# A Hyena spectrum stage on one core: each PSUM evacuation and product over two or four neighbouring banks in one instruction

## The reference, cut to what matters

```python
def long_conv(u, hf, bias):
    seqlen = u.shape[1]
    uf = jnp.fft.rfft(u, n=2 * seqlen, axis=1)
    y = jnp.fft.irfft(uf * hf[None], n=2 * seqlen, axis=1)[:, :seqlen]
    return y + u * bias

def hyena(p, lp, rows, row_len):
    ...
    hf = hyena_filters(seqlen, lp)
    z = x1 * long_conv(v, hf[:, 0], bias[0])
    z = x2 * long_conv(z, hf[:, 1], bias[1])
    return z * jax.nn.silu(p['z_b'].astype(f32))
```

## Time and profile before

| what | value |
|---|---|
| median of 3 runs | 5350.56 us (5349.45 to 5352.09) |
| the profiled execution's own time | 5330.26 us |
| its span | 5328.6 us |
| mean granted TensorE clock | 0.962 of full speed |
| busy share of the span: PE, DVE, ACT, POOL | 89%, 36%, 24%, 21% |
| matmuls | 27121 |

### The profile page before, as it was taken

One profiled execution on the slowest core, in us unless ns is written; L12 is line 12 of the kernel. 1 busy time (PEld: TensorE's weight loads), 2 busy tenths in 40 slices (PEclk: granted clock), 3 DMA queues, 4 the chain that ended last, 5 costly groups with the idle time before them and its releaser, 6 DMA issues. The chain is left out here.

```text
span 5328.6 us, 66000 instructions
## 1 busy us (share of the span) xinstructions
PE 4738.9 (89%) x27121; PEld 2951.7 (55%) x27121; DVE 1942.2 (36%) x2790; ACT 1264.8 (24%) x2707; POOL 1109.5 (21%) x1071
## 2 busy tenths in 40 slices
PE   6237999999999999999999799988888888499998
PEld 6113555555444444444444688876665555377676
DVE  0462333344862122100200466655555555212121
ACT  0101122211101111100110355545455454000000
POOL 0000000000000000000000899954333533011111
PEclk9968999999999999999999899999999999699999
DMA  2603113321341111122111777755454544713130
GB/s 105 206 0 127 43 48 88 81 62 52 105 114 56 52 55 59 48 101 79 60 47 55 220 210 210 207 161 195 152 196 160 185 172 152 261 64 126 63 126 24
DMA packets 440191, 602.92 MB, mean 113 GB/s; under 512 B 123536, under 2 KB 355400, under 8 KB 416968
## 3 DMA queue, kind: packets, MB, share of 16 engines
q1 hardware_dynamic: 407368, 530.79, 30.5%
q0 software_dynamic: 14112, 51.39, 3.5%
q10 hardware_dynamic: 18432, 16.79, 0.9%
HBM read 377.17 MB, written 221.70 MB: 112 GB/s over the span
## 5 line engine op out<-in xcount | busy, mean ns | idle before, releaser
L1002 PE MATMUL proj_b<-proj_hT,proj_wt 128*128 128x512 f32 (+1 forms) x5504 | 2312.5, 581 | 1.0 <-issue 0.7
L1002 PEld LDWEIGHTS proj_b<-proj_hT,proj_wt 128*128 128x128 f32 x5504 | 1047.5, 191 | 1213.2 <-issue 1201.9
L615 POOL DMA_DIRECT2D proj_wt<-in_w_in_dram x80 | 71.3, 892 | 2588.7 <-PE proj_b L1002 2401.5
L747 ACT ACTIVATE proj_rawx<-proj_b 128x512 f32<-128x512 f32 x192 | 114.8, 600 | 949.5 <-PE proj_b L1002 908.8
L749 ACT ACTIVATE proj_res<-proj_b 128x512 f32<-128x512 f32 x128 | 76.5, 597 | 788.0 <-PE proj_b L1002 788.0
L2241 PE MATMUL mrg_b<-mrg_za,mrg_w_a 128*128 128x256 f32 x1024 | 233.6, 381 | 27.4 <-DMA mrg_w_o<-in_w_out_dram 27.4
L860 DVE TENSOR_SCALAR proj_arena<-proj_rawx,proj_cw_hy 128x2048 f32<-128x2048 f32 x24 | 32.3, 1346 | 561.9 <-PE proj_b L1032 515.2
L2241 PE MATMUL mrg_b<-mrg_yb,mrg_w_b 128*128 128x256 f32 x1024 | 231.5, 379 | 0.0
L2254 PE MATMUL mrg_b<-mrg_w_o,mrg_mt 128*128 128x512 f32 x512 | 221.9, 594 | 6.6 <-POOL mrg_mt L2127 6.6
L2241 PEld LDWEIGHTS mrg_b<-mrg_za,mrg_w_a 128*128 128x128 f32 x1024 | 195.4, 191 | 57.4 <-issue 31.1
L2241 PEld LDWEIGHTS mrg_b<-mrg_yb,mrg_w_b 128*128 128x128 f32 x1024 | 194.6, 190 | 26.5
(11 more groups left out here) (268 smaller groups left out, 6310.7 us busy)
## 6 DMA issues: line engine op xcount, KB each, us to landing
proj_wt<-in_w_in_dram POOLq DMA_DIRECT2D x80, 512.0 KB, 5.1
delta_kq<-scratch_KQ SPq DMA_DIRECT2D x144, 256.0 KB, 4.1
delta_nv<-scratch_NV SPq DMA_DIRECT2D x144, 256.0 KB, 4.0
scratch_bounce_f<-fft_first SPq DMA_DIRECT2D x32, 1024.0 KB, 3.8
fft_yf<-scratch_bounce_f SPq DMA_DIRECT2D x32, 1024.0 KB, 6.0
scratch_bounce_i<-fft_yi SPq DMA_DIRECT2D x32, 1024.0 KB, 4.5
fft_second<-scratch_bounce_i SPq DMA_DIRECT2D x32, 1024.0 KB, 8.6
scratch_hy<-proj_arena SPq DMA_DIRECT2D x24, 1024.0 KB, 4.7
```

Of the source, the lines that this page charges most:

```text
L747: ins = act.activation(rawx[:, r0:r0 + width // ROW, 2:2 + ROW], src.rearrange("p (r t) -> p r t", t=ROW), ACT.Copy)
L1002: last = pe.matmul(main[g][:, 0:width], wt[:, i % 2, k, :], hT[:, k, first:first + width], start=(k == 0), stop=(k == KT - 1))
```

## The change

The 8 banks become one PSUM tensor, so that neighbouring banks can be one operand. S now takes 4 places of the plan in place of one (three of them hold nothing), so that every group of 4 starts at bank 0 or 4. T is read in two pairs of banks: 0 and 1 by ACT, 2 and 3 by DVE. X, R, M and I are read 4 banks at a time. Each wide instruction waits for the last of its banks, and counts up by 2 or 4 when it is done. The matmuls, the DMAs and their order are as before. So are the other readers (filters, D, O, Z).

```diff
-        banks = kit.banks("b", 8)
+        psum = ctx.enter_context(nc.psum_tensor("fft_b", [P, 8, 512], F32))
+        banks = [psum[:, i, :] for i in range(8)]
...
-                        use(*[("S", t, 0)])
+                        use(*[("S", t, i) for i in range(4)])
...
+        def side_by_side(*name, count):
+            i = index[name] % 8
+            return psum[:, i:i + count, :].rearrange("p i x -> p (i x)")
...
                 def empty_turn(t, s):
-                    for i in (0, 2):
-                        ready(act, "T", t, 4 * s + i)
-                        act.activation(yd[:, i, :], bank("T", t, 4 * s + i)[:, :], ACT.Copy).then_inc(emptied["act"], 1)
+                    ready(act, "T", t, 4 * s + 1)
+                    act.activation(row(yd[:, 0:2, :]), side_by_side("T", t, 4 * s, count=2), ACT.Copy).then_inc(emptied["act"], 2)
 
                 def empty_data_spectrum(t, s):
-                    for i in range(4):
-                        ready(act, "X", t, 4 * s + i)
-                        if i == 0 and s:
-                            read(act, "M", t, 4 * s - 1)
-                        act.activation(xs[:, i, :], bank("X", t, 4 * s + i)[:, :], ACT.Copy).then_inc(emptied["act"], 1)
+                    ready(act, "X", t, 4 * s + 3)
+                    if s:
+                        read(act, "M", t, 4 * s - 1)
+                    act.activation(row(xs), side_by_side("X", t, 4 * s, count=4), ACT.Copy).then_inc(emptied["act"], 4)
 
                 def empty_inverse(t, s):
-                    for i in range(4):
-                        ready(act, "I", t, 4 * s + i)
-                        if i == 0:
-                            wait(act, i_written, 16 * (4 * t + s))
-                        act.activation(yi[:, 2 * i:2 * i + 2, :].rearrange("p g c -> p (g c)"), bank("I", t, 4 * s + i)[:, :], ACT.Copy).then_inc(emptied["act"], 1)
+                    ready(act, "I", t, 4 * s + 3)
+                    wait(act, i_written, 16 * (4 * t + s))
+                    act.activation(yi[:, :, :].rearrange("p g c -> p (g c)"), side_by_side("I", t, 4 * s, count=4), ACT.Copy).then_inc(emptied["act"], 4)
...
                 def empty_turn(t, s):
-                    for i in (1, 3):
-                        ready(dve, "T", t, 4 * s + i)
-                        dve.tensor_copy(yd[:, i, :], bank("T", t, 4 * s + i)[:, :]).then_inc(emptied["dve"], 1)
+                    ready(dve, "T", t, 4 * s + 3)
+                    dve.tensor_copy(row(yd[:, 2:4, :]), side_by_side("T", t, 4 * s + 2, count=2)).then_inc(emptied["dve"], 2)
 
                 def products(t, s):
                     for kind, dst in (("R", pre), ("M", pim)):
-                        for i in range(4):
-                            ready(dve, kind, t, 4 * s + i)
-                            read(dve, "X", t, 4 * s + i)
-                            if i == 0 and s:
-                                ready(dve, "I", t, 4 * s - 1)
-                            dve.tensor_tensor(dst[:, i, :], bank(kind, t, 4 * s + i)[:, :], xs[:, i, :], ALU.mult).then_inc(emptied["dve"], 1)
+                        ready(dve, kind, t, 4 * s + 3)
+                        read(dve, "X", t, 4 * s + 3)
+                        if s:
+                            ready(dve, "I", t, 4 * s - 1)
+                        dve.tensor_tensor(row(dst), side_by_side(kind, t, 4 * s, count=4), row(xs), ALU.mult).then_inc(emptied["dve"], 4)
```

More of the change, by code:

```diff
@@ L1479, in hyena @@
         yd, xs, pre, pim = (second[:, 2048 * j:2048 * (j + 1)].rearrange("p (i x) -> p i x", i=4) for j in range(4))
+        row = lambda ap: ap.rearrange("p i x -> p (i x)")
         yt = ga[:, :, :, :].rearrange("p b n c -> p b (n c)")
-        banks = kit.banks("b", 8)
+        psum = ctx.enter_context(nc.psum_tensor("fft_b", [P, 8, 512], F32))
+        banks = [psum[:, i, :] for i in range(8)]
         plan, reads = [], []
@@ L1524, in reader @@
             kind, _, n = bank_use
-            if kind in ("A", "D", "T", "Z"):
+            if kind in ("A", "D", "Z"):
                 return "dve" if n % 2 else "act"
+            if kind == "T":
+                return "dve" if n % 4 >= 2 else "act"
             return {"hx": "dve", "hy": "dve", "O": "dve", "R": "dve", "M": "dve", "X": "act", "I": "act", "S": "act"}[kind]
@@ L1723, in _ @@
                             if s == 0:
-                                ready(act, "S", t, 0)
+                                ready(act, "S", t, 3)
                                 wait(act, gated, 3 * t)
-                                act.activation(norm[:, :], bank("S", t, 0)[:, 0:CB], ACT.Sqrt, bias=eps[:, 0:1]).then_inc(emptied["act"], 1)
+                                act.activation(norm[:, :], bank("S", t, 0)[:, 0:CB], ACT.Sqrt, bias=eps[:, 0:1]).then_inc(emptied["act"], 4)
                             if s:
@@ L1740, in sums @@
                             if t:
-                                ready(pool, "S", t - 1, 0)
+                                ready(pool, "S", t - 1, 3)
                             pool.tensor_copy(acc[:, :], sq[:, 0, :]).then_inc(added, 1)
@@ L1849, in _ @@
                             if s == 0:
-                                read(dve, "S", t, 0)
+                                read(dve, "S", t, 3)
                                 dve.reciprocal(norm[:, :], norm[:, :]).then_inc(normed, 1)
@@ L1939, in spectrum @@
                 def spectrum(t, s):
-                    read(pe, "T", t, 4 * s + 2)
+                    read(pe, "T", t, 4 * s + 1)
                     read(pe, "T", t, 4 * s + 3)
@@ L1959, in energy @@
                 def energy(t):
-                    b = take("S", t, 0)
+                    b = [take("S", t, i) for i in range(4)][0]
                     pe.wait_ge(added, 2 * PAIR * (t + 1))
@@ L1963, in energy @@
                         last = pe.matmul(b[:, 0:CB], ones[:, :], acc[:, h * CB:(h + 1) * CB], start=(h == 0), stop=(h == 1))
-                    last.then_inc(filled, 1)
+                    last.then_inc(filled, 4)
                 def results(cb):
```

## The result

| | before | after |
|---|---|---|
| median of 14 runs each, same chip | 5345.11 us (5334.97 to 5352.09) | 5360.92 us (5350.62 to 5372.11) |
| ratio of the times | | 1.0032, 95% interval 1.0023 to 1.0042 |
| span of the profiled execution | 5328.6 us | 5370.3 us |
| mean granted clock in it | 0.962 | 0.954 |

The change makes the kernel slower by 0.32%, about 17 us by the ratio (the two medians lie 15.8 us apart). The time is inside the range, but the difference is beyond the 0.2% that I called none: the forecast of +0.6 us was 16 too low. That the time is inside is partly luck. The range stood on the first three runs' median of 5350.56 us and ended 13.4 us above it; the fourteen runs' median of the kernel before is 5.4 us lower. On 5350.56 the measured ratio gives 5367.7, outside.

What follows compares the result with a forecast made beforehand. A chain of waits was taken to bound the spectrum loop, with PE the bound behind it. Terms -2.6 + 4.6 - 1.4 = +0.6 us on the median of 5350.56 gave 5351.2 us, range 5340 to 5364.

Steps and rivals of the forecast that it cites:

- Durations: Wide instructions in the spectrum loop: 2.29 us on VectorE, 1.89 on ScalarE for 2048 columns; two products 4.50, not 4.87.
- A: Rival, faster: each removed instruction saves a larger fixed cost, 0.145 us on VectorE, 0.17 on ScalarE; 5312 us, chance 0.12.
- B: Rival, slower: an instruction over four banks pays each bank as before and saves nothing; +23 us, 5374, chance 0.13.
- (1): Spectrum turns s = 1 to 3: product starts 0.26 us later, products 0.37 shorter; -0.11 in 24 turns, -2.6 us.
- (2): Same turns: transposes lose their head start but still end before the inverse can start, cover down to 0.36 us.
- C: Rival, slower: new PE idle ahead of the transposes lets the clock fall; +1.04 us in 24 turns, 5376, chance 0.04.
- (3): Turn s = 0, 8 in all: product starts 0.87 us later, products 0.30 shorter; +0.57 each, +4.6 us.
- (4): Last copy of I in a step, ahead of the table load: 1.89 us for 2.07; -0.18 in 8, -1.4 us.
- (5): S taking four places, SP's and POOL's work, and the waits: nothing added on the chain.

Runs made afterwards that it cites:

- e10: The changed kernel with every wide instruction, and S, counting up by 1 for its whole group; ratio 1.0023 to the kernel before.
- e1: The kernel before in one PSUM tensor with S taking four places, all else bank by bank; ratio 1.0018.
- e9: e1 with the root of S counting up by 1 in place of 4, the four places kept; ratio 0.9995.
- e6: The changed kernel with PE waiting once for each four banks and VectorE's doubled waits left out; 5358.47 us to 5344.87 before.
- e7: e1 with PE waiting once for each group of four banks; ratio 1.0000 to the kernel before.
- e2: e1 with only the products R and M in one instruction of four banks each; 5371.41 us to 5344.87 before.
- e12: The changed kernel with R bank by bank, one PE wait and one count for each group; 5353.57 us to 5345.44 before.

## Why the prediction was right in its durations and wrong in its sum

By its steps, with what 8 loops make of each:

- **Durations: right**, within 0.02 us. Products 4.49 for 4.50. The assumption that crossing a bank costs nothing extra and that a removed instruction saves 0.06 us on VectorE held, so A and B are both out. The Trainium skill's 125 ns (Perfetto Trace Analysis, Optimizing Scalar/DVE Operations) would have given products of 4.12; they took 4.49. The Trainium skill's other rule in that section, that smaller instructions can let work finish sooner where others wait, pointed the right way: 13 us by it alone against about 17 measured.
- **(1) Turns s = 1 to 3: mis-sized**, -0.11 forecast, +0.16 measured, from one copy of I to the next, so in place of -2.6 us +3.8. Two terms failed. I took 0.04 for the hand-over from X's copy to the product, from a pair where the waiter carries its wait itself; it was 0.21 (3676.99 to 3677.20). With counts of 1 (e10) it is 0.09, and the product stands at +3.73, my 3.74; that match is partly luck, as X's copy ended at +3.64 and not at +3.70. And I let I's copy start where it had started; it starts 0.18 later (2.50 for 2.32), of which e10 takes 0.05 away. The 0.13 left is the price of waiting for I's last bank in place of its first: in the trace PE's counts for the four banks come 0.04 us apart, and the copy starts 0.02 behind the one that it waits for.
- **(2) The cover of the transposes: right as a rule and failed by C.** They started at +6.19 (6.17 forecast). In turns at full clock they end at 3681.51, 0.18 us ahead of the products, and the inverse doesn't wait for them. In turns at half clock it does, and such a turn is 1.1 to 1.5 us longer.
- **(3) Turn 0: mechanism right, size off**, +0.57 forecast, +1.04 measured, 8.3 us for 4.6. The product came 1.37 late instead of 0.87, the products saved 0.31. The half us lies in the hand-overs: T's pair copy to X's products (0.25, before 0.10), X's products to its copy (0.31, before 0.12), the copy to the product (0.13, 0.04 forecast).
- **(4) The last copy of I**: 1.88 for 2.07 as forecast; it starts 0.18 late, so it gives nothing.
- **(5) failed outright**: "S takes four places ... Nothing. ... The waits cost nothing on the chain." I asked which banks the waits wait for, and not which instruction carries them. Alone it costs 0.72 x 8 = 5.8 us, 1.0018 (e1), and nothing when the count is 1 (e9). In the changed kernel it isn't 5.8 us on top: there T's pair copy and X's wide copy cover most of it, and with all counts at 1 turn 0 is 0.16 shorter (e10).
- **Rival C** was given 0.04 as something of all 24 turns. It came true in part: undisturbed turns make 8.3 + 3.8 = 12.1 of the 18.5 us. Of the other 6.4, most falls in the four turns whose transposes met the half clock, 4.9 us, and in the last inverses of each step, 2.5 us longer in all, 30 us of them at half clock against 25. Turns whose copy of I came late, most likely for SP's write, stand on both sides: one here (+2.0 us), two before (+1.6 and +1.1). The mechanism is the one that I named; "gaps of 1.39 left the clock alone" was the wrong reason to discount it: those gaps stood ahead of the inverse, these ahead of the transposes.

So the fall was not in the hardware's price of a wide instruction, which I spent most of the working on, but in what lies around it: the start at the last bank, hand-overs on the chain that are 0.1 to 0.2 us longer, in every turn, and a clock that answers to where the idle lies. The chance of slower, 0.18, was put mainly on B. Left open is why the clock falls in one turn and not in the next of the same shape: in e6 it does so once in each loop, in the changed kernel in four turns of 24, and no run changed that alone.

## What to carry to other kernels

Merging evacuations pays about 0.06 us per instruction here, and only where its consumer would have waited for the last piece anyway: M alone wide gains 0.20 us a turn, R or X wide loses more by the overlap than it saves. When several buffers are released at once, let the reader count once (by 1) and the waiter wait once, since both the larger count and the row of waits put time on the chain that no busy row shows. The second holds without any merging: the kernel before paid it too. And before opening a gap ahead of PE's work, look at which work would run at half clock if the gap lets it fall, and how much cover that work has.

## What the runs showed of the hardware

- An instruction of VectorE or ScalarE that counts up by more than 1 doesn't carry its wait: a wait instruction stands ahead of it instead, and of the table load that belongs to it. 0.72 us per turn 0 (e1 against e9), 0.16 us per turn of wide instructions (after against e10).
- Five waits of PE on one semaphore in the source, two wait instructions and a wait on the first weight load in the trace, cost 0.20 us more than one wait (e1 10.94, e7 10.74), 0.1 for each wait instruction, whether one count meets them (changed kernel, 0.26 us from the last product to the inverse) or four counts one after another (e1, 0.26).
- An instruction over four banks took no longer than one of the same width from SBUF: 2286 ns for 2048 columns on VectorE, 1876 on ScalarE, against 2296 for 2052 columns and 1910 for 2048 from SBUF.
- The granted clock fell to its half level for whole groups of transposes in some of the turns whose PE had 1 to 1.3 us of idle between M and the transposes (4 of 24 in the changed kernel, 8 of 24 in e6), and once in e2 behind 0.63 us; with no idle there (e12) it stayed through all transposes, though the idle ahead of the inverse was then 1.54 us. Where idle lies mattered, not only its length.
